# First mixer of a two-layer trunk: cubic term a step later, three gate-weight remainders on GpSimd, gate and rounding by two tiles, TensorE's last products reordered

## What is computed

```python
u = (h @ w_in)                                    # 272 x 1024
bu = einsum(u, Bbar)                              # complex, per group of 16 channels, 64 states
x_t = Abar * x_{t-1} + bu_t                       # scan over time
y = Re(C x) + d_skip * u
g = jax.nn.gelu(y)                                # tanh form: needs y * (1 + 0.044715 y^2)
z = g * jax.nn.sigmoid(g @ w_glu + b_glu)
return z @ w_out
```

## Time and profile before

| | |
|---|---|
| median of 3 runs | 1981.93 us (1981.31 to 1986.17) |
| profiled execution, its own time | 1979.48 us |
| its span, first to last instruction | 1977.7 us (1.78 us lie around it) |
| TensorE busy | 1953.9 us (99%) |
| VectorE, ScalarE, GpSimd busy | 1178.1, 889.4, 56.1 us |
| mean granted TensorE clock | 0.998 |
| TensorE busy from 121 to 129 us | 4.75 of 8 us |
| TensorE busy from 129 to 141 us | 10.66 of 12 us, clock 0.86 |

### The profile page before, as it was taken

How to read it: one execution, slowest core, us unless ns; L and a number is a source line. 1 busy time by engine, 2 the same in 40 slices (tenths; PEclk the granted TensorE clock), 3 DMA queues, 4 the chain that set the end, 5 groups by cost and what they waited for, 6 DMA issues and landing times.

```text
span 1977.7 us, 34357 instructions
## 1 busy us (share of the span) xinstructions
PE 1953.9 (99%) x13997; PEld 1806.5 (91%) x13997; DVE 1178.1 (60%) x1295; ACT 889.4 (45%) x1080; POOL 56.1 (3%) x66
## 2 busy tenths in 40 slices
PE   9999999999999999999999999999999999999999
PEld 7879999999999999999998989988888888888887
DVE  8887655545454545454767877555556555565554
ACT  5535543343343343333555665534444434344443
POOL 4220000000000000000000000000000000000000
PEclk9999999999999999999999999999999999999999
DMA  6225595555555555555544435555655565655654
GB/s 172 65 94 176 166 236 179 175 173 177 172 173 179 171 176 176 171 175 177 172 138 148 129 128 174 168 192 168 202 186 190 172 204 187 192 186 177 201 187 154
DMA packets 196730, 338.07 MB, mean 171 GB/s; under 512 B 19544, under 2 KB 38616, under 8 KB 196520
## 3 DMA queue, kind: packets, MB, share of 16 engines
q1 hardware_dynamic: 182616, 332.21, 52.3%
q10 hardware_dynamic: 12896, 2.83, 1.0%
q0 software_dynamic: 1088, 1.06, 0.2%
HBM read 333.48 MB, written 2.14 MB: 170 GB/s over the span
## 4 chain that ended last, share of the span: by engine, by line
PE 93%; DVE 5%; issue 1%; ACT 1%; DMA 0%; POOL 0%; SPq 0%; ACTq 0%; DVEq 0%
PE acc L295 49%; PE acc L451 18%; PE acc L410 12%; PE acc L412 6%; PE acc L715 2%; DVE wlo L277 1%; PE acc L699 1%; PE acc L831 1%; PE acc L847 0%; DVE small L1751 0%; PE acc L807 0%; DVE s_sb L1746 0%; PE acc L790 0%; PE acc L440 0%; PE acc L673 0%
## 5 line engine op out<-in xcount | busy, mean ns | idle before, releaser
L277 DVE TENSOR_TENSOR wlo<-raw,whi 128x1024 fp32r<-128x1024 f32 x608 | 738.5, 1223 | 594.3 <-ACT whi L272 594.0
L272 ACT ACTIVATE whi<-raw 128x1024 fp32r<-128x1024 f32 x608 | 639.6, 1059 | 923.4 <-PE acc L295 553.4
L295 PE MATMUL acc<-hg_hi,whi 128*128 128x272 f32 (+1 forms) x1344 | 389.0, 289 | 3.6 <-issue 1.4
L295 PE MATMUL acc<-hg_hi,wlo 128*128 128x272 f32 (+1 forms) x1344 | 386.8, 288 | 0.0
L295 PE MATMUL acc<-hg_lo,whi 128*128 128x272 f32 (+1 forms) x1344 | 384.6, 286 | 0.0
L410 PE MATMUL acc<-hg,whi 128*128 128x512 f32 x1024 | 359.7, 394 | 0.0
L295 PE MATMUL acc<-a_hi,whi 128*128 128x272 f32 x1152 | 332.8, 289 | 1.4 <-DVE a_lo L1686 1.4
L295 PE MATMUL acc<-a_hi,wlo 128*128 128x272 f32 x1152 | 333.7, 290 | 0.0
L295 PE MATMUL acc<-a_lo,whi 128*128 128x272 f32 x1152 | 331.5, 288 | 0.0
L412 PE MATMUL acc<-hg,wlo 128*128 128x256 f32 x1024 | 288.2, 281 | 0.0
L295 PEld LDWEIGHTS acc<-hg_hi,whi 128*128 128x128 f32 x1344 | 252.8, 188 | 7.5 <-issue 4.8
(11 more groups left out here) (320 smaller groups left out, 1787.5 us busy)
## 6 DMA issues: line engine op xcount, KB each, us to landing
raw<-in_mlp_w SPq DMA_DIRECT2D x512, 512.0 KB, 3.7
raw<-in_attn_w_qkv SPq DMA_DIRECT2D x40, 512.0 KB, 3.9
raw<-in_attn_w_o SPq DMA_DIRECT2D x32, 512.0 KB, 4.1
raw<-in_s_w_in SPq DMA_DIRECT2D x16, 512.0 KB, 4.2
raw<-in_s_w_out SPq DMA_DIRECT2D x16, 512.0 KB, 4.2
raw<-in_s_w_glu SPq DMA_DIRECT2D x8, 512.0 KB, 3.6
xs<-in_x SPq DMA_DIRECT2D x8, 256.0 KB, 8.2
bias_w<-bias_by_distance ACTq DMA_DIRECT2D x2, 1024.0 KB, 12.1
```

What stands on the lines that cost most here:

```text
L272: nc.scalar.activation(whi[:, k, :, :], raw[:, k, :, :], ACT.Copy).then_inc(sem("hi_split"), 1)
L277: nc.vector.tensor_tensor(wlo[:, k, :, :], raw[:, k, :, :], whi[:, k, :, :], ALU.subtract).then_inc(sem("lo_split"), 1)
L295: m = nc.tensor.matmul(o, w[:, k, t, 128 * n:128 * n + 128], xx[:, kt + t, cols], start=first and t == 0 and j == 0 and not (packed and n ...
```

## The change

`responses` is cut: the 6 matmuls of three tiles come ahead of `s5_in(0)`, the rest behind it. On VectorE `s5_cubic` of tile s-2 now stands in step s behind the rotation, `s5_gelu` behind the scan, and `u_out(s+1)` at the step's end (for tile 7 inside step 6's scan). GpSimd makes the remainders of gate halves 0, 1, 2. ScalarE's `decays` move ahead of Square, and its rounding of the gate halves 1 and 2 moves. TensorE's last products have another order. The gate's Tanh, product, rounding and remainder go by two tiles, and the splits of `w_glu` and `w_out` halves 7 and 11 stand behind them.

```diff
@@ -780,18 +780,23 @@
-                m.then_inc(sem("kd_tr"), 1)
+            def responses(power, tiles, last=False):
+
+                if tiles.start == 0 and power == 0:
+                    pe.wait_ge(sem("u_out"), 1)
+                    pe.wait_ge(sem("bp_ready"), 2)
+                    pe.wait_ge(sem("cc_out"), 2)
+                if power == 1:
+                    pe.wait_ge(sem("wb_ready"), 4)
+                for i in tiles:
+                    o = acc[:, power, 64 * i:64 * i + 64]
...
+                if last:
+                    m.then_inc(sem("kd_tr"), 1)
@@ -849,31 +854,38 @@
+            responses(0, range(3))
             s5_in(0)
-            responses()
+            responses(0, range(3, CT))
+            responses(1, range(CT), last=True)
             s5_in(1)
             in_half(6)
-            beside = {1: (7, 8), 2: (9, 10), 3: (11, 12), 4: (13, 14), 5: (15,), 6: ()}
-            for i in range(1, CT - 1):
+            beside = {1: (7, 8), 2: (9, 10), 3: (11, 12), 4: (13, 14), 5: (15,)}
+            for i in range(1, CT - 2):
                 s5_in(i + 1)
                 s5_out(i - 1)
                 for k in beside[i]:
                     in_half(k)
+            s5_out(CT - 3)
+            s5_in(CT - 1)
             glu_part(0, 0)
             s5_out(CT - 2)
             glu_part(0, 2)
-            s5_out(CT - 1)
-            for j in (1, 2, 3):
+            for j in (1, 2):
                 glu_part(j, 0)
+                if j == 2:
+                    s5_out(CT - 1)
                 glu_part(j, 2)
+            glu_part(3, 0)
+            glu_part(3, 2)
 
 
             pe.wait_ge(sem("g_ready"), CT)
             mm_group(pe, H_GLU + 4, None, G_GLU + 1, None, g_hi, g_lo, 4, ALLT)
             for g in range(4):
                 def ready(j):
-                    if g == 0 and j % 2 == 0:
-                        pe.wait_ge(sem("z_ready"), j // 2 + 1)
+                    if g == 0:
+                        pe.wait_ge(sem("z_ready"), j + 1)
                 mm_group(pe, H_OUT + 4 * g, None, G_OUT + g, None, a_hi, a_lo, 4, ALLT, ready)
@@ -1159,36 +1171,39 @@
-            SPLIT_AT = {4: 0, 5: 1, 6: 2}
+            SPLIT_AT = {4: (0, 1), 5: (2,)}
             for i in range(CT):
                 if i == CT - 1:
                     act.wait_ge(sem("zc_last"), 1)
                     split_hi(act, 3)
+                if i + 2 < CT:
+                    decays(i + 2)
                 act.wait_ge(sem("y_ready"), i + 1)
...
-                if i + 2 < CT:
-                    decays(i + 2)
                 if i in SPLIT_AT:
-                    act.wait_ge(sem("zc_ready"), i + 1)
-                    split_hi(act, SPLIT_AT[i])
+                    act.wait_ge(sem("zc_ready"), 5 if i == 4 else CT - 1)
+                    for k in SPLIT_AT[i]:
+                        split_hi(act, k)
...
             for j in range(8):
-                split_hi(act, H_GLU + j + RING)
                 if j % 4 == 3:
                     g = j // 4
                     act.wait_ge(sem("half_used"), H_GLU + j + 1)
                     if g:
-                        act.wait_ge(sem("z_ready"), g)
+                        act.wait_ge(sem("z_ready"), 2 * g)
...
+                        op = nc.scalar.activation(rbuf[:, n, :], acc[:, 4 * ((G_GLU + g) % 2) + n, 0:L], ACT.Tanh,
+                                                  scale=0.5, bias=hbglu[:, 4 * g + n:4 * g + n + 1])
+                        if n % 2:
+                            op.then_inc(sem("glu_tanh"), 1)
+                    for q in range(2):
+                        act.wait_ge(*((sem("group_out"), G_GLU + g + 1) if q else (sem("gate_out"), g + 1)))
+                        nc.scalar.activation(a_hi[:, 4 * g + 2 * q:4 * g + 2 * q + 2, :], rbuf[:, 2 * q:2 * q + 2, :], ACT.Copy,
+                                             scale=0.5).then_inc(sem("z_hi_ready"), 1)
+                split_hi(act, H_GLU + j + RING)
@@ -1325,6 +1340,13 @@
+
+            def gate_low(k, read):
+
+                pool.wait_ge(sem("zs_ready"), read)
+                pool.wait_ge(sem("hi_split"), k + 1)
+                tt(wlo[:, k, :, :], raw[:, k, :, :], whi[:, k, :, :], ALU.subtract).then_inc(sem("lo_split"), 1)
...
                 tt(zc[i % 2][:, :, :], z[i % 2][:, :, :], twice(cosb, i),
                    ALU.mult).then_inc(sem("zc_ready"), 1)
+                if i == CT - 3:
+                    gate_low(0, 3)
+            gate_low(1, 5)
+            gate_low(2, CT - 1)
@@ -1605,6 +1631,8 @@
                 link(tt(rot[:, 1, :], rot[:, 1, :], zz[:, 0, :], ALU.subtract))
+                if i == CT - 2:
+                    u_out(CT - 1)
                 dve.wait_ge(sem("decay_ready"), i + 1)
@@ -1651,40 +1679,40 @@
-                if 2 <= s < CT - 1:
-                    u_out(s + 1)
+                if s >= 2:
+                    s5_cubic(s - 2)
+                if s < CT:
+                    scan(s)
                 if s >= 2:
                     s5_gelu(s - 2)
                 if s < CT:
-                    scan(s)
-                if s == CT + 1:
-                    split_lo(dve, 3)
+                    rotate_out(s)
                 if s >= 2:
                     s5_low(s - 2)
-                if s < CT:
-                    rotate_out(s)
-                if s == 6:
-                    split_lo(dve, 0)
-                if 1 <= s <= CT:
-                    s5_cubic(s - 1)
-                if s in (7, 8):
-                    split_lo(dve, s - 6)
+                if 2 <= s < CT - 2:
+                    u_out(s + 1)
+                if s == CT:
+                    dve.wait_ge(sem("lo_split"), 3)
+                    split_lo(dve, 3)
 
...
-                split_lo(dve, H_GLU + j + RING)
                 if j % 4 == 3:
                     g = j // 4
...
+                    for q in range(2):
+                        part = slice(2 * q, 2 * q + 2)
+                        dve.wait_ge(sem("glu_tanh"), 2 * g + q + 1)
+                        stt(out=rbuf[:, part, :], in0=rbuf[:, part, :], scalar=1.0, in1=asq[:, part, :],
+                            op0=ALU.add, op1=ALU.mult).then_inc(sem("group_out") if q else sem("gate_out"), 1)
+                    for q in range(2):
+                        dve.wait_ge(sem("z_hi_ready"), 2 * g + q + 1)
+                        tiles = slice(4 * g + 2 * q, 4 * g + 2 * q + 2)
+                        stt(out=a_lo[:, tiles, :], in0=rbuf[:, 2 * q:2 * q + 2, :], scalar=0.5,
+                            in1=a_hi[:, tiles, :], op0=ALU.mult, op1=ALU.subtract).then_inc(sem("z_ready"), 1)
+                split_lo(dve, H_GLU + j + RING)
```

More of the change, by code:

```diff
@@ L781, in _ @@
                 wb_turn(k)
[L783 to L793, removed]
-                m.then_inc(sem("kd_tr"), 1)
+            def responses(power, tiles, last=False):
[7 more added lines that the diff above has]
+                    o = acc[:, power, 64 * i:64 * i + 64]
+                    for part in range(2):
+                        m = nc.tensor.matmul(o, bp[:, power, part, 128 * i:128 * i + 128],
+                                             cc[:, part, 4 * i:4 * i + 4, :],
+                                             start=part == 0 and i == 0, stop=part == 1,
+                                             skip_group_check=True)
+                if last:
+                    m.then_inc(sem("kd_tr"), 1)
             def s5_in(i):
@@ L1677, in _ @@
                     if g:
-                        dve.wait_ge(sem("z_ready"), 1)
+                        dve.wait_ge(sem("z_ready"), 2)
                     dve.wait_ge(sem("g_ready"), CT)
                     link(tt(asq[:, :, :], g_hi[:, 4 * g:4 * g + 4, :], g_lo[:, 4 * g:4 * g + 4, :], ALU.add))
-                    dve.wait_ge(sem("glu_tanh"), g + 1)
-                    stt(out=rbuf[:, :, :], in0=rbuf[:, :, :], scalar=1.0, in1=asq[:, :, :],
-                        op0=ALU.add, op1=ALU.mult).then_inc(sem("group_out"), 1)
-                    dve.wait_ge(sem("z_hi_ready"), g + 1)
-                    stt(out=a_lo[:, 4 * g:4 * g + 4, :], in0=rbuf[:, :, :], scalar=0.5,
-                        in1=a_hi[:, 4 * g:4 * g + 4, :], op0=ALU.mult, op1=ALU.subtract).then_inc(sem("z_ready"), 1)
+                    for q in range(2):
[9 more added lines that the diff above has]
+                split_lo(dve, H_GLU + j + RING)
             def residual(G, g, cols):
```

## The result

The changed kernel takes **1988.11 us** (median of 12 runs, 1986.19 to 1991.35) against 1982.85 us for the kernel before (12 runs, 1979.39 to 1986.17). The ratio is **1.0028**, 95% interval 1.0020 to 1.0036: 5.3 us slower. The forecast was 1989.3. The profiled execution's span is 1984.5 us against 1977.7, 6.8 us longer.

The account below looks back on a forecast made before the run. TensorE, busy 99%, was taken as the bound. Terms +3.8 +1.7 -3.3 +4.9 +1.7 -1.4 = +7.4 us on the 1981.93 us median gave 1989.3 us, 0.37% slower; range 1981.0 to 1992.4 us.

Parts of the forecast that it names:

- The bound: First mixer: only TensorE's four waits (6.7 us) and lost clock (1.7 us) can be won, at most about 8.4 us.
- The front: Before s5_in(0): 6 matmuls moved ahead fill 0.7 of the 1.2 us wait; what follows comes 0.7 us earlier.
- The wait for u(3): At s5_in(3): u(3), now last in step 2, makes TensorE stand 4.4 us; s5_in(3) comes 3.8 us later.
- The thin margin of the later steps: Steps 3 to 5: VectorE ends u(s+1) 0.3 us ahead of TensorE's 11.6 us pass, so no wait repeats.
- The clock: Half clock after the wait at s5_in(3) and again after that before gate part (2,0), 1.7 us lost each.
- The order of the end: Mixer's end without holds: in_half(15)'s end to the gate's first group's end takes 25.2 us, a gain of 3.3 us.
- The holds: Step 6's scan and step 7's additions: GpSimd's three remainders hold VectorE 4.9 us in all, bounds 0 to 7.2.
- The gate: Gate by two tiles: w_out's first product no longer waits for a_lo, a gain of 1.4 us.
- no hold: Mixer's end: VectorE and GpSimd hardly hold each other; sum +0.8 us, 1982.7; chance 0.22, plus 0.14 for a partial hold.
- no wait for u(3): At s5_in(3): VectorE begins step 2 earlier, so no wait; sum +1.2 us, chance 0.05.
- late in every step: Steps 2 to 5: low held by zc makes u late each step; +14.9 us, 1996.8, chance 0.07.

Follow-up runs that it names:

- a_u3: Changed kernel with u_out(3) put back behind step 2's rotation, u_out of tiles 4 to 7 still late; 1983.85 us.
- b_u3: Kernel before with only u_out(3) moved to step 2's end, in front of the cubic term; 1989.20 us, ratio 1.0032.
- a_fill2: Changed kernel with 15 unread 128x128 matmuls in TensorE's wait for u(3); 1985.80 us.
- a_fillb: Changed kernel with 18 unread 128x128 matmuls in TensorE's wait between gate parts (1,2) and (2,0); 1985.87 us.
- a_write: Changed kernel with GpSimd writing zeros in 16 short memsets per gate half instead of computing the three remainders; 1981.32 us.
- b_gate2: Kernel before with only the gate by two tiles and the splits behind it; 1980.29 us, ratio 0.9988.

## Why the prediction was right, step by step

- **The bound (waits and clock of the mixer, nothing else).** Right: the two segments and what lies behind G give the 6.8 us of the span.
- **The front.** The mechanism was right, the size wrong. I took 6 of 64 records; the 6 matmuls that move are 12 of them, since a float32 matmul is two records. (So the 64 matmuls of `responses` are 32 in the code, too.) They fill the whole wait of 1.2 us: no wait stands before `s5_in(0)`, and `s5_in(1)` starts 7.1 us behind it instead of 8.5. But the prediction has no wait behind that, and there is one: `s5_out(0)` stands 0.71 us for VectorE's `kd`. So of 1.3 us won TensorE kept 0.5 at `s5_in(3)`, where it was ready at 78.3; the forecast of 78.1 came near by two errors that cancel.
- **The wait for u(3).** Right in place and kind. 3.5 us where I had 4.4: TensorE was ready 0.2 us later than I had, and step 2 began at 72.84 and not at 73.5, since the tables came earlier by that same error, and its pieces up to `u` took 8.5 us where I had 8.64. `s5_in(3)` came 3.0 us later than before, I had 3.8. a_u3 and b_u3 show the cause from both sides.
- **The thin margin of the later steps.** It held in the changed kernel: the pass from `s5_in(3)` to `s5_in(4)` is 13.1 us, 1.5 more than the next two of 11.6, and that is the clock, with no wait. But it held only because TensorE was late: in a_u3 0.74 us of it failed at `s5_in(4)`.
- **The clock.** 1.7 us each time was the forecast, from a stretch at half clock of 3.4 us in the kernel before (130.2 to 133.6 us, inside). The first fall cost 1.5 (a_fill2), for a stretch of the same 3.4 us. The second cost 2.5 (a_fillb) and is the term that was too small: its stretch was twice as long, 6.8 us, of which 5.7 lay in work.
- **The order of the end.** E + 25.2 without holds was the sum; a_write, which has none, gave 25.2.
- **The holds.** 4.9 us was the sum; scan 0.4 and additions 4.1 make 4.5, and the segment of a_fillb, holds without a fall of the clock, is 4.6 longer than that of a_write. That GpSimd's reads are the reason is shown by a_write and the long memset beside VectorE's remainders. One premise was read too strongly: "both overlaps shown were paid nearly in full" holds for the first (0.9 us of 1.06), but at L1537 the overlap was 0.28 us (65.90 to 66.18) and 0.09 were paid, a third, so that of the two rows only the first bears out a hold for the other's whole length. The long overlaps of step 7 did: 2.1 us (134.12 to 136.20) made the first addition 1.9 us longer, 2.3 (136.70 to 139.04) the second 2.2. On the reads, the page "SBUF — State Buffer" of the Trainium skill says the same in "Who interferes with whom", and adds that a GpSimd instruction that only writes doesn't contend with two SBUF inputs; the memsets of this case agree with that too (0.71 us for an addition beside them).
- **The gate.** 1.4 us, shown alone by b_gate2 (1.3 us there, 1.6 in the changed kernel, from G to the end).

Sum: I had +5.5, +3.3, -1.4, in all +7.4; it was +4.54, +3.80, -1.57, in all +6.8 on the spans. The mechanisms were right, but that the total is nearer than its first part is luck: the errors were of opposite sign. That the medians differ by 5.3 us and the two profiled executions by 6.8 is not explained by a run; the start-up and the length of the slow stretch both scatter, and the interval of the ratio, 4.0 to 7.1 us, holds both figures. I expected slower by over 0.3% with a chance of 0.53 and within with 0.43; at 0.28% the median lies just inside, and the runs can't tell which side is true.

Of the rivals, "no hold" falls by the two additions and a_write, "no wait for u(3)" by the row at 81.81, "late in every step" by the passes of 11.6 us behind it.

## What to carry to other kernels

When instructions are moved within one engine's written order, ask for each what another engine waits for: here one 0.43 us instruction, moved from the head of a step to its end, cost TensorE 3.5 us and its clock. Work given to GpSimd isn't free for VectorE where both then read two operands from SBUF: 3.7 us taken off VectorE cost it 4.5. Look for a wait of the engine that is full before handing its work to another: two of the three remainders fitted into one, but for 0.75 us. And a gain that sits in the same diff as a loss (1.4 us of the gate) is only seen when it is run alone.

## What the runs showed of the hardware

- An addition of 0.72 us on VectorE took 2.65 and 2.92 us beside GpSimd's two-operand instructions, and 0.71 beside its memsets. GpSimd was held by VectorE as well: the second remainder took 2.90 us, the first 2.41. A VectorE remainder of 1.22 us kept its time beside a single GpSimd memset of 1.49 us.
- Behind a wait of 3.5 us TensorE's clock was at half for 3.4 us; at one of 4.6 us for 6.8 us in three kernels, of which 0.7 to 2.1 us fell into the wait itself, and for 3.4 us in two (a_fill2, b_u3). A microsecond of this in TensorE's work cost 0.44 to 0.45 us. Unread matmuls in either wait kept the clock at 1.00 and gave back 1.5 and 2.5 us.
- A float32 matmul of 128x128 is two records of 0.115 us; a group's count in the profile is not the count in the code.
- The start of the mixer lay between 53.65 and 59.05 us in twelve profiled executions with nearly the same instructions ahead of it (the changed order has six matmuls more there); the kernel before and the changed one, 53.65 and 53.68, hardly differ. That scatter is as large as the whole effect of this change.
